# Hybrid MLA and Mamba-2 block on one core: input projection by K tiles, the kv norm behind the values, and the SSD convolution with tiles taken in ahead

## What is computed

```python
def mla_mixer(hx, hc, row, col, w_in, q_norm, w_uq, kv_norm, w_ukv, w_o, need_ctx):
    h = jnp.concatenate([hc, hx], axis=1)
    proj = h @ w_in
    cq, ckv, kr = jnp.split(proj, [Q_LORA, Q_LORA + KV_LORA], axis=-1)
    q = (rms_norm(cq, q_norm) @ w_uq).reshape(bsz, T, MLA_HEADS, QK_NOPE + QK_ROPE)
    kv = (rms_norm(ckv, kv_norm) @ w_ukv).reshape(bsz, T, MLA_HEADS, QK_NOPE + V_HEAD)
    ...
def ssd_mixer(...):
    proj = jnp.concatenate([hc, hx], axis=1) @ w_in
    z, xbc, dt_raw = jnp.split(proj, [SSD_INNER, SSD_INNER + SSD_CONV_DIM], axis=-1)
    xbc = jax.nn.silu(dw_conv(xbc, conv_w, conv_b))
    ...
```

## Time and profile before

| | us |
|---|---|
| median of 3 runs | 1237.01 (1235.58 to 1238.70) |
| the profiled execution | 1236.16 |
| its span, first to last instruction | 1234.4 |
| PE busy | 1159.1 (94%) |
| DVE busy | 878.1 (71%) |
| ACT busy | 623.3 (50%) |
| GpSimd busy | 217.3 (18%) |

### The profile page before, as it was taken

How to read it: one execution, slowest core, us unless ns; L and a number is a source line. 1 busy time by engine, 2 the same in 40 slices (tenths; PEclk the granted TensorE clock), 3 DMA queues, 4 the chain that set the end, 5 groups by cost and what they waited for, 6 DMA issues and landing times.

```text
span 1234.4 us, 19406 instructions
## 1 busy us (share of the span) xinstructions
PE 1159.1 (94%) x6954; PEld 970.9 (79%) x6954; DVE 878.1 (71%) x1340; ACT 623.3 (50%) x1056; POOL 217.3 (18%) x162
## 2 busy tenths in 40 slices
PE   5799999888999999999999879998999899999996
PEld 3577676678988888888888868886677799999996
DVE  0896888976787777776665588885988756666654
ACT  3646888734532222232222556447677456666642
POOL 0201445422100000000111100004777200000010
PEclk9899999999999999999999989999999899999999
DMA  9534132240465655564452132321212344555572
GB/s 381 193 121 135 52 103 87 69 164 8 171 224 186 203 189 170 186 211 162 162 166 67 58 103 87 100 85 35 79 59 68 103 137 164 171 176 170 165 216 65
DMA packets 48176, 168.23 MB, mean 136 GB/s; under 512 B 5232, under 2 KB 6512, under 8 KB 47856
## 3 DMA queue, kind: packets, MB, share of 16 engines
q1 hardware_dynamic: 48112, 167.38, 41.2%
HBM read 166.31 MB, written 1.05 MB: 136 GB/s over the span
## 4 chain that ended last, share of the span: by engine, by line
PE 65%; DVE 18%; ACT 9%; issue 5%; DMA 1%; POOL 1%; DVEq 0%; ACTq 0%; SPq 0%
PE bank L1737 19%; PE bank L1739 19%; PE bank L1738 19%; DVE scratch L1479 5%; DVE w_lo L1108 3%; ACT w_hi L609 2%; PE bank L2164 2%; DMA ada_start<-in_ada_w 1%; PE bank L2197 1%; ACT scratch L914 1%; DVE softmax_max L1279 1%; PE bank L2176 1%; ACT conv_in L911 1%; PE bank L2186 1%; DVE mla_h_lo L1299 1%
## 5 line engine op out<-in xcount | busy, mean ns | idle before, releaser
L1108 DVE TENSOR_TENSOR w_lo<-raw,w_hi 128x1024 fp32r<-128x1024 f32 (+1 forms) x226 | 277.1, 1228 | 133.4 <-ACT w_hi L609 133.2
L609 ACT ACTIVATE w_hi<-raw 128x1024 fp32r<-128x1024 f32 (+1 forms) x226 | 230.3, 1021 | 240.8 <-PE bank L1739 217.7
L1737 PE MATMUL bank<-ffn_h_lo,w_hi 128*128 128x258 f32 (+2 forms) x736 | 246.0, 334 | 5.7 <-DVE ffn_h_lo L1382 2.3
L1739 PE MATMUL bank<-ffn_h_hi,w_lo 128*128 128x258 f32 (+2 forms) x736 | 244.5, 332 | 0.0
L1738 PE MATMUL bank<-ffn_h_hi,w_hi 128*128 128x258 f32 (+2 forms) x736 | 244.4, 332 | 0.0
L1737 PEld LDWEIGHTS bank<-ffn_h_lo,w_hi 128*128 128x128 f32 x736 | 139.4, 189 | 21.9 <-DVE ffn_h_lo L1382 2.7
L1738 PEld LDWEIGHTS bank<-ffn_h_hi,w_hi 128*128 128x128 f32 x736 | 139.2, 189 | 14.5
L1739 PEld LDWEIGHTS bank<-ffn_h_hi,w_lo 128*128 128x128 f32 x736 | 138.9, 189 | 14.7
L465 POOL TENSOR_TENSOR scratch<-scratch 128x512 f32<-128x512 f32 (+1 forms) x24 | 34.1, 1419 | 618.3 <-ACT scratch L618 618.3
L1737 PE MATMUL bank<-ssd_h_lo,w_hi 128*128 128x256 f32 (+2 forms) x360 | 126.0, 350 | 12.4 <-DVE w_lo L1108 10.1
L1737 PE MATMUL bank<-ffn_hidden_lo,w_hi 128*128 128x256 f32 (+1 forms) x374 | 123.6, 330 | 1.0 <-DVE ffn_hidden_lo L1691 0.9
(11 more groups left out here) (275 smaller groups left out, 2185.6 us busy)
## 6 DMA issues: line engine op xcount, KB each, us to landing
raw<-in_w SPq DMA_DIRECT2D x120, 512.0 KB, 4.3
scratch<-in_vec_w SPq DMA_DIRECT2D x56, 512.0 KB, 3.5
vec_weights<-in_vec_w SPq DMA_DIRECT2D x24, 512.0 KB, 3.6
raw<-in_w_xbc SPq DMA_DIRECT2D x24, 512.0 KB, 3.5
ada_start<-in_ada_w SPq DMA_DIRECT2D x8, 1024.0 KB, 17.2
raw<-in_w_z SPq DMA_DIRECT2D x16, 512.0 KB, 3.5
raw<-in_w_so SPq DMA_DIRECT2D x16, 512.0 KB, 3.6
raw<-in_w SPq DMA_DIRECT2D x16, 384.0 KB, 4.5
```

What stands on the lines that cost most here:

```text
L609: A(wh[s % RING][:, 0:c], raw[s % RING][:, 0:c], ACT.Copy).then_inc(w_hi, 1)
L1108: V.tensor_tensor(wl[s % RING][:, 0:c], raw[s % RING][:, 0:c], wh[s % RING][:, 0:c].bitcast(f32), SUB).then_inc(w_lo, 1)
L1737: mm(o, lh, rl, start=first, stop=False)
L1739: return mm(o, ll, rh, start=False, stop=final)
```

## The change

**First stage.** `w_in` is cut by K: block `IN + k` holds the 128 input features of tile k for all seven output tiles (896 columns), and `in_all(k)` makes 21 matmuls into seven banks at once. The modulation weights are laid out anew, so that one group gives shift and scale of two K tiles (`start_mods(q)`), and PE's queue interleaves groups, turns and `in_all`. `X` is loaded first, in two halves, and its squares are summed ahead of everything else. K tiles 6 and 7 are done last, one output tile after the other. The value product takes the kv tiles with their gains but without their norm (`cgh`, `cgl`), and ACT multiplies each token's row by `v_scale` on the way out; the normed kv tiles, which the K blocks need, are made later (`norm(1, ...)` at t == 6). Three matvecs stand before the kv tiles' low parts in DVE's queue, and five behind the norm.

**SSD.** ACT's queue takes in tile t before the SiLU of tile t - 1, splits of the weights are given by `conv_splits`, the turned tiles are copied out by ACT (not DVE) three tiles later, four banks take the x tiles in turn, and the loops are written out. `cumulated` and `c_times_b` (the sums of dtA and the C x B products) move between x tiles. GpSimd weighs x for states 0 and 1 and makes `backward(0)` during tiles 16 to 21. Behind the last tile come states(0) and two z tiles, then the turns of tiles 22 and 23.

```diff
-VEC_IN = (0, 1, 2, 4, 5)
+VEC_IN = 3
...
+def conv_splits(t):
...
+    first = ([BC + 4, BC + 5], [BC + 6, BC + 7], [DT], [XS], [XS + 1], [XS + 2], [XS + 3], [])
+    return first[t] if t < 8 else [XS + t - 4]
...
+            for i in range(2):
+                sp.dma_start(X[:, 4 * i:4 * i + 4, :], a["xT"][:, 4 * i:4 * i + 4, :]).then_inc(x_in[i], 16)
             ada_start(0)
             sp.dma_start(tab[:, :], a["tab"]).then_inc(inputs_in, 16)
             ada_start(1)
-            sp.dma_start(X[:, :, :], a["xT"]).then_inc(x_in, 16)
             ada_start(2)
             ada_start(3)
+            load(IN, IN, 896, one("w_in", 0))
+            load(IN + 1, IN + 1, 896, one("w_in", 1))
...
+            for t in range(2):
                 vec(2 + t, vec_mla[:, t, :])
...
+            pool.wait_ge(w6_done, 3)
+            pool.wait_ge(conv_ev, 8)
+            weigh_x(0, (17, 18, 18))
+            weigh_x(1, (19, 20, 20))
+            pool.wait_ge(conv_y, 21)
+            pool.wait_ge(cb_done, 4)
+            backward(0)
             pool.wait_ge(w_used, ZS)
             pool.wait_ge(dt_dve, 12)
             mask_forward(0)
...
+                if t == 4:
                     act.wait_ge(kr_done, 1)
                     rms(1, TOK, 128 * KKV)
...
+            for t in range(24):
+                taken(t)
+                if t == 1:
+                    splits(1)
+                if t:
+                    conv_silu(t - 1)
+                if t in (3, 4, 6, 8):
+                    to_tokens((3, 4, 6, 8).index(t))
...
+                if t >= 11:
+                    to_tokens(t - 3)
+                if t != 1:
+                    splits(t)
...
+            dve.wait_ge(inv, 1)
+            for q in range(4):
+                start_mods(q)
+                start_value(2 * q)
+                if q == 0:
+                    lo(IN, IN)
+                start_low(2 * q)
+                start_low(2 * q + 1)
...
+            lo(VB, VB)
+            lo(VB + 1, VB + 1)
+            dve.wait_ge(crow_silu, 1)
+            for v in range(VEC_IN):
+                matvec_mla(v)
...
+                if t == 6:
                     whole = [(0, 0, TOK)]
...
+            lo(VB + 2, VB + 2)
+            lo(VB + 3, VB + 3)
+            for v in range(VEC_IN, VEC_HEADS):
...
+            def in_all(k):
...
+                pe.wait_ge(w_lo, IN + k + 1)
+                pe.wait_ge(nlo, k + 1)
+                for t in range(7):
+                    if k == 0 and t >= 4:
+                        pe.wait_ge(*((row_cp, t - 3) if t < 6 else (root, 1)))
+                    last = in_part(k, t)
+                last.then_inc(w_used, 1)
...
+            ada_group(0)
+            pe.wait_ge(inputs_in, 16)
+            turn_ready(0)
+            turn()
+            ada_group(1)
+            in_all(0)
+            turn_ready(1)
+            turn()
+            in_all(1)
+            ada_group(2)
+            in_all(2)
...
+            in_all(5)
+            pe.wait_ge(w_lo, IN + KD)
+            for t in range(7):
+                for k in (6, 7):
...
+            conv_tile(4)
+            conv_tile(5)
+            to_tokens(0)
+            conv_tile(6)
+            conv_tile(7)
+            to_tokens(1)
+            pe.wait_ge(conv_up, 3)
             pe.wait_ge(w_lo, DT + 1)
...
+            to_tokens(2)
+            conv_tile(8)
+            to_tokens(3)
+            for t in range(9, 24):
+                conv_tile(t)
+                if t >= 11:
+                    to_tokens(t - 3)
...
+                if t == 11:
+                    c_times_b()
+                if t == 15:
+                    cumulated()
+            to_tokens(21)
...
+            pe.wait_ge(conv_up, 24)
+            pe.wait_ge(cb_done, 4)
+            states(0)
+            pe.wait_ge(cum_exp, 1)
+            z_tile(0)
+            z_tile(1)
+            to_tokens(22)
+            to_tokens(23)
+            decay(0, 0)
+            decay(0, 1)
```

557 lines of the change are left out of this document (310 added, 247 removed).

## The result

| | before | after |
|---|---|---|
| median, us | 1237.7 (1235.6 to 1238.7) | 1220.6 (1220.35 to 1221.26) |
| the profiled execution | 1236.16 | 1220.4 |
| its span | 1234.4 | 1218.6 |
| PE busy | 1159.1 (94%) | 1159.0 (95%) |

The ratio is 0.9869, with a 95% interval from 0.9856 to 0.9881. A second measurement gave 1219.4 us and 0.9861 [0.9846, 0.9876]. The forecast was 1223 us. PE's busy time is the same, so the 15.8 us of span that went are idle time of PE (75.3 us before, 59.6 after). Matmuls are called cold here when they run at the lower level of TensorE's clock, which the profile's rows show as a granted clock of 0.50.

A forecast was written before the change was run, and what follows sets the result against it. PE bounds the kernel where it is fed, DVE where it isn't, and the start waits for bytes. 10.2 + 5.6 - 1.5 = 14.3 us gained gives 1223 us; own range 1218 to 1228, 8 in 10 from 1211 to 1231.

The forecast's parts named there:

- Part 1: Convolution's first tiles, 698 to 730: paired splits and earlier taking in remove PE's idle time and cold matmuls; gain 10.2 us.
- the 0.3 I had kept: Convolution's first tiles: one PE wait of 0.3 us counted as remaining, and none after.
- the one slow tile: Convolution tile begun at 720.93: 24 matmuls took 4.40 us at the lower clock, need 2.8; 1.6 us more.
- Part 2: The x tiles: PE's load is unchanged without idle time, the change only adds cover; cost 0, at most 3 us.
- Part 3: Behind the last x tile: all PE waits covered, also one in the loop, and clock loss avoided; gain 5.6 us.
- named waits: PE's waits for a turned tile's copy, a state and a weighed x, together 3.48 us; a mask, 0.75.
- Part 4: First stage up to the values: first product at 25.8 us, values at 76.9, 10.7 us earlier.
- The 2.4 us of cold matmuls that I kept: First stage: 12 matmuls at 0.44 us after PE's waits before its first product; without them 2.4 us more won.
- Part 5: DVE's queue behind the values: block A's product at 105.5, head 0's scores at 112.5 against 110.72.
- a loss of 1.5: Whole first stage: head 0's scores later by 1.8 us, rounded to a loss of 1.5.
- Rival 1: The first stage's gain passes, as matvecs may slip in sooner: 1209 us; chance 0.17.
- Rival 2: Half of the convolution's gain is lost, ACT late with a split and PE waiting in C tiles: 1230 us; chance 0.15.

The follow-up runs named there:

- threefold kernel: Each of GpSimd's six weighings of x done three times over during the tiles, against the changed kernel: 1222.2 us, ratio 0.9882.
- the queue is cleared: Changed kernel with w_heads loads issued earlier, block A's split behind the second of five matvecs, the fifth moved into the heads: 1212.2 us; one step further, 1211.0 us.
- either half of part 1 undone: Against the changed kernel: taking in of the next tile put back behind the SiLU, 1223.5 us; splits put back to one a tile behind the taps, 1227.3 us.

## Why the prediction was right, and which of its terms were not

The time, 1220.6 against 1223, is within the forecast's own range. By its steps:

**Part 1, predicted 10.2, measured 12.0** (10.8 at the dt product, and the kernel was 1.2 late at 677). The idle time went as said, without the 0.3 I had kept. Two turns, some 0.9 us, now stand behind the dt product. What is left, 12.0 less 8.8 less 0.9, is 2.3 us. Of that the clock holds some 1.4. It was low twice between the norm and the dt product: right behind the norm, as it still is, and from 717.4 to 724.2, of which PE was at work only in this stretch of the kernel before (PE's busy time, clock, DMA share, GB/s):

```profile
720.93:724.23 3.30, 3.30 (x15) 0.50 0.53 159
```

The 15 matmuls stand 0.21 us apart, and 0.12 at full clock. So the one slow tile, priced at 1.6 us, was all of it. The last 0.9 us is likely the ends of the four waits that are gone, an estimate: the matmul ahead of a wait counts with its whole 0.28 us and not with the 0.12 to the next, and the first behind one is followed 0.1 us later than others (711.09 to 711.31). That was not measured apart.

**Part 2, predicted 0, measured 0.** PE is busy for 25.00 of 25 us from 795 to 820. Groups of four taps took 3.8 to 4.6 us beside one or two GpSimd operations in place of 3.1. It even bears three times the weighing within the tiles. My row for the price was of two taps beside a mask, 1.6 us lost for 1.9 of GpSimd, which makes DVE's need 28 us and not the 29 I wrote; 0.7 to 1.5 us a group is the measured loss. The cover that ACT's copies, the four banks and the moved sums give was not undone one by one. By the exclusive lock of the Trainium skill (SBUF, section "SBUF: two separate sides") DVE and GpSimd together could do no more than 23.0 us of their own work in the 23.0 us from 795.53 to 818.55 of the threefold kernel. DVE did 12 taps and 3 splits, 12 x 0.75 + 3 x 1.22 = 12.7 us undisturbed, and GpSimd's weighings, 1.55 us apart (18 from 791.57 to 819.49), make 14.8, at 1.04 each undisturbed (before, at 846.66) 15.4: 28 us in 23. So the trace agrees that they slow each other, and not that one of them stands still for the whole instruction.

**Part 3, predicted 5.6, measured 5.7 up to the loop's end** (16.5 ahead at 954.78, where before it was 971.33, less 10.8). All named waits are gone. But what I gave as the reason for the turns' place, the two z tiles, is wrong: one does as well. The first state, ready early, does the work; the weighing alone is worth about 2 us. Some 0.8 us were given back by the end: the lead is 16.6 us at 961.58, 16.2 at 978.61 and 15.8 at 1152.10. What took it isn't shown.

**Part 4, predicted 25.8 and 76.9, measured 26.25 and 75.22.** The stretch between took 49.0 us, not 51.1. The range of outcomes here is the clock's: 72.9 to 73.8 in six of eleven traces. The 2.4 us of cold matmuls that I kept were 1.4 to 1.6 in the five others and none in the six. That the clock would fall behind PE's waits of over 2 us held in all (the one of 2.77 us); that it would still be low at the first product was near even odds, and in this trace luck.

**Part 5, predicted block A 28.6 us behind the values and the scores 7.0 behind it, measured 28.45 and 6.5.** The queue was told instruction by instruction, and right: the idle time 7.8 and not 10, because PE was through the K and C blocks 20.6 us behind the start of the values and not 18.6, with the clock low from 83.9 to 87.3, which is some 1.5 us of it. In the second trace, with the clock full there, it was through at 19.1 and stood idle for 8.86. The step from there, that the whole first stage is a loss of 1.5, is off by 1.8: alone, it is even with the kernel before. The fall of 1.45 us in the heads was in no term of mine.

**The sum.** 10.2 + 5.6 - 1.5 = 14.3 was forecast; 17.2 and 0.3 were measured one by one, 17.1 together. Rival 1 had the right outcome for a kernel that wasn't this one: when the queue is cleared, 8 to 10 us of the first stage's 12 do pass, and 1211 us is what it gives. Rival 2 named late splits as the danger, and either half of part 1 undone shows it, by DVE's low parts (3 to 7 us).

## What to carry to other kernels

A stage that is made faster hands its gain on only if no other engine's queue stands between it and the next stage: write out, per engine, what is queued behind the stage and who waits for the first thing in it. Work that nobody waits for (here modulations needed 200 us later) belongs behind what the bound engine needs next, and so do its loads in the DMA queue and its conversions in the third engine's. And where a wait of one or two microseconds on the matrix engine is won or lost, count the cold matmuls behind it as well: they were some 1.4 us of part 1's 12.0, 1.45 us behind a wait of 1.87 in the heads, and 2.7 behind one of 3.05. And before the clock is blamed on a wait, look whether it had fallen already.

## What the runs showed of the hardware

- PE's clock is not a matter of the last wait's length alone. At the start it fell before the last wait in all 12 traces with the changed first stage (20.6 to 23.5 us), and the length of that wait, 1.01 to 1.98 us, followed from when it had fallen. It was back before the first product in six and 2.9 to 3.4 us behind it in five, which cost 1.4 to 1.6 us; with PE at work in the wait it was back before the product too, in one trace.
- In the heads, one and the same wait of 1.86 to 1.89 us was followed by full clock in four traces (0.39 us a matmul of 512 columns) and by the low one in ten (0.63 us, from 210.2 to 213.6 in the changed kernel's first): 1.45 us. Of two executions of one kernel, the clock may differ at the start, as in the two of the changed kernel. In six traces it fell near 83 us with no wait of PE before it.
- DVE with two SBUF inputs beside GpSimd all the time: 0.75 to 1.42 us a tap and 1.22 to 2.06 a split, while GpSimd's weighing went from 1.04 to 1.53. Together they did 1.2 times what they could have done in turn (28 us of work in 23.0).
- Ten matmuls of ones by ones, 128 columns, fp32, took 3.3 us, with the clock at 0.50 for the first 2.2, so a filling meant to last 1 us lasted three times that.
